# Low parts written in place over the raw weights, six high buffers, expert blocks of 512 columns, and expert rows gathered channel by channel

## The reference

```python
def swiglu(x, wg, wu, wd):
    return jnp.dot(jax.nn.silu(jnp.dot(x, wg)) * jnp.dot(x, wu), wd)

def moe_swiglu(x, router, wg, wu, wd):
    logits = jnp.dot(xf, router)
    top_v, top_i = lax.top_k(logits, TOP_K)
    probs = jax.nn.softmax(top_v, axis=-1)
    gate = jnp.sum(jax.nn.one_hot(top_i, N_EXPERTS) * probs[..., None], axis=1)
    for e in range(N_EXPERTS):
        y = y + gate[:, e:e + 1] * swiglu(xf, wg[e], wu[e], wd[e])
```

## Time and profile before

| | |
|---|---|
| median of 3 runs | 1303.0 us (1302.25 to 1303.61) |
| the profiled execution | 1302.67 us, span 1300.9 us |
| granted TensorE clock, mean | 0.992 of full speed |
| PE busy | 1243.0 us, 96% of the span |
| PE weight loads | 1158.3 us, 89% |
| DVE busy | 1027.0 us, 79% |
| ACT busy | 825.3 us, 63% |
| DMA | 332.65 MB, 256 GB/s over the span |

### The profile page before, as it was taken

How to read it: one execution, slowest core, us unless ns; L and a number is a source line. 1 busy time by engine, 2 the same in 40 slices (tenths; PEclk the granted TensorE clock), 3 DMA queues, 4 the chain that set the end, 5 groups by cost and what they waited for, 6 DMA issues and landing times.

```text
span 1300.9 us, 22335 instructions
## 1 busy us (share of the span) xinstructions
PE 1243.0 (96%) x8651; PEld 1158.3 (89%) x8651; DVE 1027.0 (79%) x1064; ACT 825.3 (63%) x979; POOL 5.4 (0%) x22
## 2 busy tenths in 40 slices
PE   6999999999998899999999999999999999999992
PEld 4899999989988689989989989989998999998991
DVE  6687444467996688888888888889889879888886
ACT  3636563344876657767767767767776776776771
POOL 0000000000000000000000000000000000000000
PEclk9999999999999999999999999999999999999997
DMA  9355544422565169989989989999999998998931
GB/s 252 98 167 177 154 153 155 147 85 65 174 216 182 65 212 366 362 280 366 365 276 361 364 292 352 364 316 322 365 322 318 367 353 284 367 362 278 367 117 38
DMA packets 249537, 332.65 MB, mean 256 GB/s; under 512 B 6404, under 2 KB 222820, under 8 KB 249450
## 3 DMA queue, kind: packets, MB, share of 16 engines
q1 hardware_dynamic: 249283, 331.28, 75.8%
q10 hardware_dynamic: 199, 0.62, 0.2%
HBM read 330.44 MB, written 2.84 MB: 256 GB/s over the span
## 4 chain that ended last, share of the span: by engine, by line
PE 84%; DVE 10%; ACT 3%; issue 2%; DMA 0%; DVEq 0%; SPq 0%; ACTq 0%
PE bank L1088 36%; PE bank L1108 19%; PE bank L915 17%; PE bank L946 6%; DVE cacc L1368 2%; PE bank L1052 2%; PE bank L1097 1%; PE bank L1073 1%; ACT w_hi L546 1%; PE bank L854 1%; DVE acc L1533 1%; PE bank L900 1%; DVE sg L1265 1%; DVE yy_lo L1583 1%; DVE w_lo L1185 1%
## 5 line engine op out<-in xcount | busy, mean ns | idle before, releaser
L1185 DVE TENSOR_TENSOR w_lo<-raw,w_hi 128x2048 fp32r<-128x2048 f32 x309 | 707.8, 2291 | 184.3 <-ACT w_hi L546 183.6
L546 ACT CAST w_hi<-raw 128x2048 fp32r<-128x2048 f32 x309 | 591.1, 1914 | 226.1 <-PE bank L915 76.5
L1088 PE MATMUL bank<-w_hi,xg_hi 128*128 128x256 f32 x1408 | 400.7, 285 | 5.5 <-DVE acc L1533 3.7
L1088 PE MATMUL bank<-w_hi,xg_lo 128*128 128x256 f32 x1408 | 393.3, 279 | 0.0
L1088 PE MATMUL bank<-w_lo,xg_hi 128*128 128x256 f32 x1408 | 393.1, 279 | 0.0
L1088 PEld LDWEIGHTS bank<-w_hi,xg_hi 128*128 128x128 f32 x1408 | 264.5, 188 | 13.3 <-issue 9.1
L1088 PEld LDWEIGHTS bank<-w_lo,xg_hi 128*128 128x128 f32 x1408 | 265.0, 188 | 3.2
L1088 PEld LDWEIGHTS bank<-w_hi,xg_lo 128*128 128x128 f32 x1408 | 264.2, 188 | 0.0
L915 PE MATMUL bank<-x_hi,w_hi 128*128 128x304 f32 (+1 forms) x544 | 166.0, 305 | 6.9 <-DVE x_lo L1272 3.6
L915 PE MATMUL bank<-x_hi,w_lo 128*128 128x304 f32 (+1 forms) x544 | 164.0, 302 | 0.0
L915 PE MATMUL bank<-x_lo,w_hi 128*128 128x304 f32 (+1 forms) x544 | 163.2, 300 | 0.0
(11 more groups left out here) (202 smaller groups left out, 1279.5 us busy)
## 6 DMA issues: line engine op xcount, KB each, us to landing
raw<-in_moe_w_gate_dram SPq DMA_DIRECT2D x88, 1024.0 KB, 5.6
raw<-in_moe_w_up_dram SPq DMA_DIRECT2D x88, 1024.0 KB, 6.0
raw<-in_moe_w_down_dram SPq DMA_DIRECT2D x88, 1024.0 KB, 5.2
raw<-in_conv_w_dram SPq DMA_DIRECT2D x12, 1024.0 KB, 5.6
raw<-in_ffn_w_gate_dram SPq DMA_DIRECT2D x11, 1024.0 KB, 5.3
raw<-in_ffn_w_up_dram SPq DMA_DIRECT2D x11, 1024.0 KB, 5.4
raw<-in_ffn_w_down_dram SPq DMA_DIRECT2D x11, 1024.0 KB, 4.9
poolw<-in_pool_w_dram SPq DMA_DIRECT2D x1, 1024.0 KB, 10.8
```

Source lines behind the costliest of these rows:

```text
L546: act.copy(w_hi[t % SPLIT][:], raw[raw_slot(t)][:]).then_inc(hi_ready, 1)
L1088: last = pe.matmul(bank[:, 0:TW], x[:, c, :], w[:, c, :], start=(c == 0 and k == 0), stop=(c == KC - 1 and k == 2))
L1185: dve.tensor_tensor(w_lo[t % SPLIT][:], raw[raw_slot(t)][:], w_hi[t % SPLIT][:], ALU.subtract).then_inc(split_ready, 1)
```

## The change

Low parts are written over the raw tile they come from, so the 48 KB that held three pairs hold six high buffers (HIGH = 6), and a raw buffer comes free when PE has used its tile. An expert's gate and up are done in NB = 6 blocks, five of 512 columns and one of 256; a gate or up tile of a wide block is half the channels (4 chunks) by 512 columns, with DRAM rows of 2 KB (`quad`), so such a block has two gate and two up tiles and, behind them, two down tiles of the block before. `lo` runs AHEAD = 5 tiles in front, and `one_expert` is written out for two experts in one turn of the loop. The gather makes `xg` directly with channels on the partitions, 48 matmuls of 128 columns, with the rows as weights and `sel` as the moving operand; `rows_evac` and `gather_turn` are gone. The gate and up blocks and the scatter have swapped banks to suit. `g_row` and `b_row`, used by the last norm, are loaded at the end into the place of `xg` and not early into a place of their own.

```diff
-SPLIT = 3
+HIGH = 6
+        w_lo = [at(f"w_lo{i}", [P, 2048], F32R, ring_at + 8192 * i) for i in range(RAW)]
+        w_hi = [at(f"w_hi{i}", [P, 2048], F32R, split_at + 8192 * i) for i in range(HIGH)]
+        FIRST = [0] + [6 * b - 2 for b in range(1, NB)]
-        AHEAD = 3
+        AHEAD = 5
+        EARLY_TILES = 3
-        SCATTER_BANKS = (1, 4, 5, 3, 6, 7)
+        SCATTER_BANKS = (0, 4, 5, 2, 6, 7)
 SP, load:
-                    sp.wait_ge(split_ready, load_ahead(t) + 1)
+                    sp.wait_ge(tile_used, load_ahead(t) + 1)
 SP, load_expert:
-                sp.wait_ge(split_ready, n * TE + (t - RAW + 1))
+                sp.wait_ge(tile_used, n * TE + (t - RAW + 1))
 SP, after the experts:
-            sp.wait_ge(acc_ready, 6)
+            sp.wait_ge(h_done, FC + E * NB)
             sp.dma_start(g_row[:], ...)
 ACT, hi:
-                    act.wait_ge(tile_used, n * TE + (t - SPLIT + 1))
-                act.copy(w_hi[t % SPLIT][:], raw[raw_slot(t)][:]).then_inc(hi_ready, 1)
+                    act.wait_ge(tile_used, n * TE + (t - HIGH + 1))
+                act.copy(w_hi[t % HIGH][:], raw[raw_slot(t)][:]).then_inc(hi_ready, 1)
 ACT, one_expert:
+                for j in range(NB):
+                    a = FIRST[j] + AHEAD
+                    ahead(a)
+                    if halves(j) == 2:
+                        ahead(a + 1)
+                    silu(j)
+                    if j:
+                        turn_evac(j - 1)
...
+                turn_evac(NB - 1)
                 if not last:
                     xg_evac(n + 1)
-                    hi(T_MOE + TE + 1, n)
-                    hi(T_MOE + TE + 2, n)
+                ahead(TE + AHEAD - 2)
+                ahead(TE + AHEAD - 1)
 PE:
-            def gather_rows(g):
-            def gather_turn(g):
+            def gather(g):
                 pe.wait_ge(sel_ready, g + 1)
                 for half in range(2):
                     for c in range(4):
                         f = (4 * half + c) * P
+                        for i in range(3):
+                            m = OUT_ROWS[i]
+                            for x in (xn_hi, xn_lo):
+                                last = pe.matmul(ps[1 + 2 * half][:, c * P:(c + 1) * P], x[0:m, i, f:f + P],
+                                                 sel[0:m, i, :], ...)
                     last.then_inc(gathered, 1)
+                def rows_block(bank, j, g):
+                    w = halves(j) * TW
+                    for half in range(halves(j)):
+                        t = m0 + g + half
+                        pe.wait_ge(split_ready, pair * TE + (t + 1))
+                        if j == 0:
+                            pe.wait_ge(xg_lo_done, n * 2 + (half + 1))
...
+                turn_h(NB - 1)
                 if not last:
-                    gather_turn(n + 1)
-                down(NJ - 1, T_MOE + TE - 1)
+                    gather(n + 1)
+                down(NB - 1, TE - 1)
 DVE, one_expert:
+                for j in range(NB):
+                    a = FIRST[j] + AHEAD
+                    ahead(a)
+                    if j == 1:
+                        add_scattered(e, r * SCAT + e * 6, range(4, 6))
+                    if halves(j) == 2:
+                        ahead(a + 1)
+                    if j:
+                        turn_low(j - 1)
+                    if halves(j) == 2:
+                        ahead(a + 2)
+                        ahead(a + 3)
+                    else:
+                        ahead(a + 1)
+                    mult(j)
+                    if j == 0:
+                        dve.wait_ge(h_done, n * NB + (FC + 1))
+                        add_scattered(e, r * SCAT + e * 6, range(4))
...
+                turn_low(NB - 1)
                 if not last:
                     xg_low(n + 1)
-                    lo(T_MOE + TE + 1, n)
-                    lo(T_MOE + TE + 2, n)
+                ahead(TE + AHEAD - 2)
+                ahead(TE + AHEAD - 1)
```

More of the change, by code:

```diff
@@ L468, in one_pass @@
             def one_pass(r):
[L469 to L473, removed]
+                with sp.Fori(0, E // 2 - 1) as d:
+                    for j in range(LENT, 2 * TE + LENT):
+                        load_expert(r * E + 2 * d, 2 * d, j)
+                for j in range(LENT, 2 * TE):
+                    load_expert(r * E + (E - 2), E - 2, j)
             one_pass(0)
-            sp.wait_ge(acc_ready, 6)
-            sp.dma_start(g_row[:], ln_ffn_g[1, :].partition_broadcast(P)).then_inc(rows_landed, 16)
-            sp.dma_start(b_row[:], ln_ffn_b[1, :].partition_broadcast(P)).then_inc(rows_landed, 16)
             sp.wait_ge(flag_ready, 1)
@@ L797, in one_pass @@
             def one_pass(r):
-                rows_evac(r * E)
                 xg_evac(r * E)
-                with act.Fori(0, E - 1) as e:
-                    one_expert(r, e, False)
-                one_expert(r, E - 1, True)
+                for j in range(EARLY_TILES, AHEAD):
+                    hi(T_MOE + j, r * E)
+                with act.Fori(0, E // 2 - 1) as d:
+                    for side in range(2):
+                        one_expert(r, 2 * d, side, False)
+                for side in range(2):
+                    one_expert(r, E - 2, side, side == 1)
             one_pass(0)
@@ L808, in _ @@
                 with act.Fori(1, 3) as r:
-                    for j in range(AHEAD):
+                    for j in range(EARLY_TILES):
                         hi(T_MOE + j, r * E)
@@ L1145, in one_expert @@
                     else:
-                        if j == NJ - 1 and not last:
-                            gather_rows(n + 1)
-                        down(j - 1, g + 2)
-                turn_h(NJ - 1)
+                        down(j - 1, g + 2 * halves(j))
+                turn_h(NB - 1)
                 if not last:
-                    gather_turn(n + 1)
-                down(NJ - 1, T_MOE + TE - 1)
+                    gather(n + 1)
+                down(NB - 1, TE - 1)
             def one_pass(r):
-                gather_rows(r * E)
-                gather_turn(r * E)
-                with pe.Fori(0, E - 1) as e:
-                    one_expert(r, e, False)
-                one_expert(r, E - 1, True)
+                gather(r * E)
+                with pe.Fori(0, E // 2 - 1) as d:
+                    for side in range(2):
+                        one_expert(r, 2 * d, side, False)
+                for side in range(2):
+                    one_expert(r, E - 2, side, side == 1)
                 scatter((r * E + E) * 2 + r + 1)
@@ L1565, in one_expert @@
                     if j == 1:
                         add_scattered(e, r * SCAT + e * 6, range(4, 6))
-                    turn_low(j - 1)
-                    lo(T_MOE + g + 3, n)
-                    mult(j, g + 1)
-                    if not last or j < NJ - 1:
-                        lo(T_MOE + g + 4, n)
+                    if halves(j) == 2:
+                        ahead(a + 1)
+                    if j:
+                        turn_low(j - 1)
+                    if halves(j) == 2:
+                        ahead(a + 2)
+                        ahead(a + 3)
+                    else:
+                        ahead(a + 1)
@@ L1586, in one_pass @@
             def one_pass(r):
-                with dve.Fori(0, E - 1) as e:
-                    one_expert(r, e, False)
-                one_expert(r, E - 1, True)
+                for j in range(EARLY_TILES, AHEAD):
+                    lo(T_MOE + j, r * E)
+                with dve.Fori(0, E // 2 - 1) as d:
+                    for side in range(2):
+                        one_expert(r, 2 * d, side, False)
+                for side in range(2):
+                    one_expert(r, E - 2, side, side == 1)
                 dve.wait_ge(summed, r * SCAT + 6 * E)
```

258 lines of the change are left out of this document (131 added, 127 removed).

## The result

The changed kernel takes 1358.7 us (median of 4 runs, 1358.1 to 1359.8), the kernel before 1303.3 in the same measurement. The ratio is 1.0413, 95% interval 1.0392 to 1.0435. The forecast was 1321, range 1303 to 1333: the sign is right, and the time is 38 us above the forecast and 26 above the range.

The account below looks back on a forecast made before the run. The prediction took PE to bound the experts (8 x 102.9 = 823 us, 63% of the time), with DVE next. Terms: -8 (wide) + 12 (gather) + 12 + 3.4 (wait for `acc`) = +19, 1322, stated as 1321; range 1303 to 1333.

Parts of the forecast that it names:

- Wide blocks: Gate and up tiles at 512 columns, 2.74 us each: -1.0 us an expert, -8 in all; bounds +0.4 and -1.8.
- The gather: Between experts: 48 matmuls of 128 columns at 0.1125, 5.4 us, 5.7 with transposes; +1.7 an expert, seven times, +12.
- both bounds, 0.059 and 0.225: Gather, us per narrow matmul: half a 256-column one (-0.9 an expert), or as slow as plain float32 (+7.1 an expert).
- the prediction's own signs of being wrong: Gather matmuls spaced other than 0.11, the wait for `acc` under 1 us, or PE or ACT waiting for `raw`.
- Where DVE is late: Block 0 behind the gather: PE waits 2.2 us for `acc`; +12 in seven experts, +3.4 in the first.
- DVE's walk of 18.9 us: From gather's end through DVE's queued `lo`, `yy_lo`, `mult(0)` and `acc` to PE's matmul: 18.9 us.
- PE's 16.7: PE's work meanwhile: one down tile, four wide tiles and the scatter, 6 x 2.74, plus 0.3: 16.7 us.
- The term of +1.7 an expert: Wait for `acc` before block 1's first gate tile: 2.2 us against 0.46 before, in seven experts, +12.
- the forecast of 105.2: Time of one expert after the change: from 102.9 to 105.2 us.
- The first gather, "zero": Ahead of the first expert: the gather grows, but PE's 1.73 us wait for the whole `xg_lo` goes: zero.
- What costs nothing: Raw buffers, loads, late `g_row` and `b_row`, doubled loop body: no cost; without cover those two loads up to 8.
- Rival 2: Gather: narrow fp32r runs at plain float32's pace, 0.225 each; 43 us more, 1364 in all. Chance 0.11.

Follow-up runs that it names:

- e10: e5 with PE's loop over pairs of experts written out, four pairs one after the other: 1287.3 us, ratio 0.9862 to the kernel before.
- e1: Changed kernel with the gather's third row block multiplied with all 128 rows (96 zeros) instead of 32: 1323.6 us, ratio 1.014 to the kernel before.
- e6: e1 with each gather block computed twice, 96 matmuls of 128 columns in a row, same output: 1373.8 us, ratio 1.0524 to the kernel before.
- e8: Kernel before with only the new gather, all 128 rows, so no switch of rows: 1321.0 us, ratio 1.0118 to the kernel before.
- e3: Kernel before with only the new gather, 32-row matmuls and row switches kept: 1367.0 us, ratio 1.0474 to the kernel before.
- e4: e1 with two of DVE's four `ahead` in block 0 moved behind `mult(0)` and the four sums: 1303.0 us, ratio 0.9982 to the kernel before.
- e2: Changed kernel with the gather of before (12 wide matmuls, copy, 8 transposes): 1313.9 us, ratio 1.0064 to the kernel before.
- e5: e2 with two of DVE's four `ahead` in block 0 moved behind `mult(0)` and the four sums: 1296.4 us, ratio 0.9943 to the kernel before.
- e7: Changed kernel, rows still switched, half the gather moved ahead of the last block's two down tiles: 1345.4 us, ratio 1.0301 to the kernel before.

## Why the prediction was wrong, step by step

**Wide blocks: right.** Four wide tiles take 10.99 us, forecast 4 x 2.74 = 10.96. e10 shows it whole: 102.9 - 100.6 = 2.3 us an expert less than before. Summed from start to start on PE's timeline, 1.4 of it are the gate and up tiles with the transposes between them (forecast 1.0, bound 1.8) and 0.8 the scatter with the old wait for `acc` (0.46 of it the wait).

**The gather: the step that failed.** The price, 48 x 0.1125 = 5.4 us, was right for the matmul that I priced, a narrow one behind one of its own shape (e1: 5.4; e6: 10.7 for 96), and both bounds, 0.059 and 0.225, were far off. (With the transposes that is 5.4 + 0.23 = 5.6, not the 5.7 of the prediction; the term is +1.6, and e8 measures +1.4.) The error was to count forty-eight equal matmuls where sixteen of them have 32 rows. Per gather it missed:

- the switches: 8 x 0.96 = 7.7 us instead of 5.4, +2.3;
- the clock inside the gather: 10.1 in the mean of seven instead of 7.7, +2.4;
- the clock in the down tile behind it: 4.9 instead of 2.8, +2.1.

Together 6.8 an expert, 48 in seven. e3 less e8, which differ in this alone, is 46.0, with 3.4 of it in the first gather. The row blocks stood in the diff, and the earlier trace rows had even a 128-row and a 32-row matmul next to each other. I used these rows for their pace and not for the step between them. The next row of that view closes the pair:

```profile
447.13 0.93 PE L1041 MATMUL bank<-taken,ones 128*128 128x8 f32 x6
```

The two 32-row records fill 447.13 - 446.82 = 0.31 us, the four 128-row ones ahead of them 0.52.

Two of the prediction's own signs of being wrong came: the gather's matmuls are not all 0.11 apart, and the wait for `acc` is under 1 us.

The Trainium skill ("TensorE: Matmul & The Clock Gate", "LDWEIGHTS (loading the stationary operand)") says that a weight load of 32 rows takes as long as one of 128. The loads themselves agree, 0.18 and 0.19 us; but the first load of another row count starts 0.15 us late, the six matmuls take 0.29 us longer by it, and the measurement decides. The 81 ns for a stream of pairs that the Trainium skill gives on that page ("Back-to-back issue gap"), which I had weighed against the row, is seen nowhere: the fastest here is 0.111.

**Where DVE is late: right in the queue, wrong in what PE does meanwhile.** DVE's walk of 18.9 us was exact in the expert shown, and 18.8 in e1. PE's 16.7 became 18.9 - 0.45 = 18.45 in the expert shown, nearly all of it by a down tile of 4.5 us where I had 2.74. The visible wait was 0.45, not 2.2. The term of +1.7 an expert was thus paid by the slow clock: with the gather's +6.8 and this one's -1.75 the forecast of 105.2 would be 110.2, measured 109.7; the 0.4 that the wide blocks gave beyond their term is most of the rest. With full rows the term is there, 2.1 us, and the order edit takes it out again (20.6 us in e4, forecast for the term 12 + 3.4, and the old 0.46 with it, 3.7: 19).

**The first gather, "zero": wrong by 6.3.** From its first matmul to the first gate matmul are 6.99 us before (449.09 to 456.08, the wait of 1.73 in it) and 13.3 after. The wait is gone, as forecast, but the gather runs at 1.2 GHz in all but its first matmuls. The same stretch in the two kernels, after and then before:

```profile
452.00:455.00 3.00, 3.00 (x12) 2.65 (x12) 0.13 (x1) 0.00 (x0) 0.00 (x0) 0.50 0.00 0
```

```profile
452.00:455.00 3.00, 1.18 (x9) 0.85 (x8) 0.50 (x2) 2.12 (x4) 0.00 (x0) 1.00 0.00 0
```

With it the 10 us missing in the first stretch are accounted for: 6.3 here, 2.4 in the four wide tiles behind it (13.4 us instead of 11.0, the clock coming back only within them), 3.6 in the gather at the stretch's end (9.0 instead of 5.4), and 2.0 back by a first wait of 1.6 instead of 3.6.

The switches are not its whole cause: with full rows it is still at half clock, some 10 us in e1 and in e8. The old gather there is at half clock in e2 and e10 (5.4 us from its first matmul to its first transpose) and at full clock in e5 and before (4.2). PE has little to do in the router ahead of it, in all of these kernels alike, and why the clock falls there in some and not in others was not settled; no run was made for it. That it stays down once it has fallen is what e6's first gather shows: the full-row narrow stream does not bring it back.

**What costs nothing: right for the loads, wrong for the loop.** No engine waits for an expert's `raw`. In the dense part ACT waits for its loads, 12 to 40 us for each matrix, but that stretch of the chain is 147.48 us long as before. For the doubled loop body I had put nothing; the chain of before could not show it, its body being half as long. It costs 0.7 and 0.2 us at the two jumps in e1 and, in e5, 3.6 and 5.4 in the two experts that meet it, 9 in all. The waits of the changed kernel show no such stop of PE, so it adds nothing there. That the code of PE comes late after the jump fits this, and so do the instruction blocks at 659 and 663 us in e5 and their absence in the loop of before. The queue does not say whose code a block is, and only the jump was taken away, so the cause of the stop is supported and not shown.

**The rivals.** None had the mechanism. Rival 2 gave 1364, near the time, by a wrong cause: the pace of plain float32. It would have shown starts 0.225 apart from the first matmul on; they are 0.11 between full-row matmuls in the first 5 us, and 0.21 only with the clock at half. e6 rules it out.

## What to carry to other kernels

When matmuls of different row counts alternate in one stream, price the alternation and look at the granted clock there, not only at the pace of one shape; padding the short ones with rows of zeros cost nothing here and gained 35 us. When a new wait is forecast behind work whose own duration is uncertain, the two terms do not add: first make the matmuls fast, then the order edit is worth twice as much. A loop body that is doubled should be tried with its loop written out before its time is put down to the work in it.

## What the hardware showed that I had not expected

- A pair of fp32r matmuls with 32 rows between pairs with 128 rows: starts 0.20, 0.17, 0.20, 0.16 us apart instead of 0.11; six take 0.96 instead of 0.67. In the weight loads it is the passage alone: 0.26 at each change of the row count, 0.11 otherwise, between two loads of 32 rows too. No run has a long stream of 32-row matmuls alone.
- The granted clock fell from 2.4 to 1.2 GHz with PE at 3.00 busy of 3 us in each window, in a stream of such switches, and stayed at 2.4 in 96 matmuls without them. Once down, it stayed at 1.2 through 18 us of those same 96 matmuls without an idle gap (e6, first gather), and was back 2 us into 512-column ones.
- PE stopped for 0.2 to 3.5 us at the jump back of a loop whose body is two experts long (e1, e2, e4, e5, e7), with nothing shown as awaited; written out, it did not. With a body of one expert the instruction queue moved nothing in 620 us; with two it moved 27 blocks of 16 KB.
